# A mixture-of-experts block whose tokens are dispatched by lists: rows gathered by index, results added into an accumulator in DRAM

## The chip, the cores and the metric

The kernel runs on one core of a Trainium2 chip. The metric is the device time of one execution, in microseconds, as the median of several runs. The core has TensorE (PE), VectorE (DVE), ScalarE (ACT), GpSimd (POOL) and SyncE (SP), which run their own instruction streams and meet through semaphores. SP, ACT and POOL issue DMAs, which 16 DMA engines carry out.

## The reference, cut to what matters

```python
def grouped_moe(x, w_router, b_router, w_gate, w_up, w_down):
    bsz, s, d = x.shape
    xt = x.reshape(bsz * s, d)
    gates = shared_group_router(xt, w_router, b_router).astype(x.dtype)
    out = jnp.zeros_like(xt)
    for e in range(N_EXPERTS):
        h = jax.nn.silu(xt @ w_gate[e]) * (xt @ w_up[e])
        out = out + gates[:, e:e + 1] * (h @ w_down[e])
    return out.reshape(bsz, s, d)

def reference(...):
        ...
        x = layer_norm(DN_ALPHA * x + merged @ w_out[l], ln1_g[l], ln1_b[l])
        moe = grouped_moe(x, w_router, b_router, w_exp_gate[l], w_exp_up[l], w_exp_down[l])
        x = layer_norm(DN_ALPHA * x + moe, ln2_g[l], ln2_b[l])
```

There are 512 tokens of width 1024, 16 experts with a hidden width of 512, float32 throughout. The router picks two experts for each token, so a row of `gates` has two entries that aren't zero. DN_ALPHA is 2 to the power 1/4. Ahead of this stand an input projection, two token mixers (a short convolution and a linear recurrence) and an output projection; `x` after the first layer norm is `x1` below.

## The kernel before

Every float32 product is made of three matmuls: a weight is split into a high part (ScalarE copies it to float32r, `whi` or `ehi`) and a low part (VectorE subtracts, `wlo` or `elo`), the data likewise, and TensorE adds high by high, high by low and low by high. So each weight tile passes DMA, ScalarE, VectorE and TensorE in this order. Everything is written out by hand: each engine has its list, and the semaphores set what waits for what.

The kernel has four stages.

1. **Projections and mixers** (lines 533 to 625 on PE): 74 weight tiles stream through two buffers `wst`. Beside them, POOL zeroes two DRAM buffers `xs` and `ys` of 23 blocks of 128 rows (lines 459 to 467): first one block of `xs` after each finished weight tile, then the parts of `ys`, whose waits have long been met by then.
2. **Output projection, layer norm, router.** DVE works out for every token its two experts and gates, and `dest`, the row that it gets in block order (block b is expert b; a block is 128 rows; further blocks would hold what an expert has over 128). `warm` (line 648) is matmuls whose result is not used, put where TensorE would otherwise wait. The rows of block 0 are made on TensorE itself, by multiplying `x1` with columns of ones and zeros, `block0` (line 754). At the same time POOL scatters the rows of `x1` to `xs` at `dest` (line 471), eight DMAs of 512 KB each, waits for them and loads block 1 (line 488).
3. **Experts.** A turn of TensorE is `gate_up(b)`, `rows_t(b + 1)` (the transposes of the next block's rows, line 710), `down(b - 1)`, `hidden_t(b)`. The rows come through one buffer `xe`, and y leaves through one buffer `yb`. ACT's turn rounds the next expert's weights and copies y out of PSUM in two halves (`y_out`, line 1032, semaphore `y_evac`), each followed by a DMA to `ys`. SP loads six weight tiles of 1 MB for each expert (line 328), one buffer `est` for each of the six; a buffer is free when the low part is made. A block's first 80 rows (`HEAD`) are loaded and stored by two DMAs, the rest only where the expert has more than 80 tokens. POOL's queue in this stage is, for b from 3: `load_rows(b)`, which waits for the transposes of the block ahead (`xe_t`), then `store_rest(b - 3)`, which waits for `y_evac`.
4. **Combination and second layer norm.** After the last store, POOL gathers each token's two rows of `ys` (line 528), TensorE sums them with `x1` by diagonal matrices of the gates and of alpha (lines 791 and 796), DVE does the layer norm from PSUM (lines 1303 to 1332), and SP stores four tiles.

## Time and profile before

| | us |
|---|---|
| median of 3 runs | 893.28 |
| lowest, highest run | 891.27, 897.67 |
| span of the profiled execution | 895.1 |
| PE busy | 856.0 (96%) |
| DVE busy | 575.7 (64%) |
| ACT busy | 465.1 (52%) |
| POOL busy | 75.4 (8%) |
| share of PE in the chain of waits | 87% |
| share of DMA in the chain of waits | 5% |

The span runs from the first to the last instruction of the core in the one execution that was profiled. Nothing is shown for that execution but its span, so the span is held against the median. Busy time is time in which an engine executes; an engine with little of it can still hold up others by where a wait stands in its list. The kernel moved 195.87 MB by DMA.

### The profile page before, as it was taken

The numbers are of one execution on the slowest core, as the hardware profiler recorded it, in microseconds if no ns is written. First come the engines' busy times: TensorE is split into PE (matmuls) and PEld (weight loads), VectorE is DVE, ScalarE is ACT, GpSimd is POOL, SyncE is SP. The second block draws the span as 40 slices with busy tenths as digits, with TensorE's granted clock in tenths as the row PEclk, the third lists the DMA queues.
The fourth block names the chain that finished last, engine by engine and source line by source line (L and its number), as shares of the span: only waits on it lengthen the run. The fifth ranks groups of instructions, "written<-read, shape, count | busy, mean of one in ns | idle before, by whom it ended". The sixth has DMA issues, their size and how long they took to land.

```text
span 895.1 us, 12524 instructions
## 1 busy us (share of the span) xinstructions
PE 856.0 (96%) x4036; PEld 709.3 (79%) x4036; DVE 575.7 (64%) x626; ACT 465.1 (52%) x482; POOL 75.4 (8%) x137
## 2 busy tenths in 40 slices
PE   6999999979999999999999999899999999999993
PEld 5888788868888888888888988688888888888761
DVE  5778344334458874423544698478889889888727
ACT  3655543423566653422325541468787877778610
POOL 1100000500000000000000001401111110010040
PEclk8999999989999999999999998899999999999997
DMA  6565555972333335334229814699999999999753
GB/s 181 175 177 166 177 196 189 251 246 89 94 94 94 94 115 170 114 100 118 88 69 335 262 41 161 255 355 372 380 373 379 383 381 372 381 381 382 256 170 135
DMA packets 168097, 195.87 MB, mean 219 GB/s; under 512 B 7998, under 2 KB 106918, under 8 KB 168070
## 3 DMA queue, kind: packets, MB, share of 16 engines
q1 hardware_dynamic: 154374, 157.69, 52.6%
q0 software_dynamic: 10624, 32.57, 10.8%
q10 hardware_dynamic: 3072, 5.24, 1.6%
q8 instruction: 17, 0.28, 0.1%
q14 instruction: 10, 0.08, 0.0%
HBM read 164.94 MB, written 30.54 MB: 218 GB/s over the span
## 4 chain that ended last, share of the span: by engine, by line
PE 87%; DMA 5%; DVE 4%; ACT 1%; POOL 1%; issue 1%; ACTq 0%; SPq 0%; DVEq 0%; POOLq 0%
PE psA L553 7%; PE psA L554 7%; PE psA L555 7%; PE psA L722 6%; PE psA L724 6%; PE psA L723 6%; PE psB L553 6%; PE psB L555 6%; PE psB L554 6%; PE psB L743 3%; PE psB L745 3%; PE psB L744 3%; PE psB L648 2%; DMA wst<-in_w_in_dram 2%; PE psD L553 2%; PE psD L554 2%
## 5 line engine op out<-in xcount | busy, mean ns | idle before, releaser
L1282 DVE TENSOR_TENSOR elo<-est,ehi 128x2048 fp32r<-128x2048 f32 x94 | 211.6, 2288 | 37.1 <-ACT ehi L964 36.8
L964 ACT ACTIVATE ehi<-est 128x2048 fp32r<-128x2048 f32 x92 | 173.3, 1914 | 38.0 <-DMA est<-in_w_exp_down_dram 16.6
L1095 DVE TENSOR_TENSOR wlo<-wst,whi 128x1024 fp32r<-128x1024 f32 (+1 forms) x78 | 97.5, 1249 | 97.5 <-ACT whi L811 96.4
L811 ACT ACTIVATE whi<-wst 128x1024 fp32r<-128x1024 f32 (+1 forms) x78 | 83.9, 1077 | 93.8 <-PE psA L555 36.4
L722 PE MATMUL psA<-ehi,xe_hi 128*128 128x512 f32 x256 | 102.2, 399 | 1.5 <-DVE xe_lo L1479 1.5
L724 PE MATMUL psA<-ehi,xe_lo 128*128 128x512 f32 x256 | 100.6, 393 | 0.0
L723 PE MATMUL psA<-elo,xe_hi 128*128 128x512 f32 x256 | 100.4, 392 | 0.0
L553 PE MATMUL psB<-xT_hi,whi 128*128 128x512 f32 x208 | 80.9, 389 | 0.0
L554 PE MATMUL psB<-xT_lo,whi 128*128 128x512 f32 x208 | 80.9, 389 | 0.0
L555 PE MATMUL psB<-xT_hi,wlo 128*128 128x512 f32 x208 | 80.9, 389 | 0.0
L722 PEld LDWEIGHTS psA<-ehi,xe_hi 128*128 128x128 f32 x256 | 48.6, 190 | 12.0 <-DVE xe_lo L1479 2.2
L553 PE MATMUL psA<-xT_hi,whi 128*128 128x512 f32 x144 | 57.4, 398 | 0.0
L554 PE MATMUL psA<-xT_lo,whi 128*128 128x512 f32 x144 | 57.1, 397 | 0.0
L555 PE MATMUL psA<-xT_hi,wlo 128*128 128x512 f32 x144 | 57.0, 396 | 0.0
L724 PEld LDWEIGHTS psA<-ehi,xe_lo 128*128 128x128 f32 x256 | 48.5, 189 | 10.5
L723 PEld LDWEIGHTS psA<-elo,xe_hi 128*128 128x128 f32 x256 | 48.6, 190 | 9.8
L743 PE MATMUL psB<-ehi,hT_hi 128*128 128x512 f32 x128 | 52.0, 406 | 1.8 <-DVE hT_lo L1491 1.8
L745 PE MATMUL psB<-ehi,hT_lo 128*128 128x512 f32 x128 | 50.8, 397 | 0.0
L744 PE MATMUL psB<-elo,hT_hi 128*128 128x512 f32 x128 | 50.4, 393 | 0.0
L553 PEld LDWEIGHTS psB<-xT_hi,whi 128*128 128x128 f32 x208 | 39.0, 188 | 8.2
L554 PEld LDWEIGHTS psB<-xT_lo,whi 128*128 128x128 f32 x208 | 39.0, 188 | 8.2
L555 PEld LDWEIGHTS psB<-xT_hi,wlo 128*128 128x128 f32 x208 | 39.0, 188 | 8.0
(271 smaller groups left out, 1630.3 us busy)
## 6 DMA issues: line engine op xcount, KB each, us to landing
est<-in_w_exp_gate_dram SPq DMA_DIRECT2D x32, 1024.0 KB, 12.2
est<-in_w_exp_up_dram SPq DMA_DIRECT2D x32, 1024.0 KB, 10.6
est<-in_w_exp_down_dram SPq DMA_DIRECT2D x32, 1024.0 KB, 11.8
wst<-in_w_in_dram SPq DMA_DIRECT2D x60, 512.0 KB, 3.9
xs<-zero POOLq DMA_DIRECT2D x23, 512.0 KB, 2.9
wst<-in_w_out_dram SPq DMA_DIRECT2D x16, 512.0 KB, 5.2
wst<-in_w_branch_r_dram SPq DMA_DIRECT2D x8, 640.0 KB, 4.2
ys<-yb ACTq DMA_DIRECT2D x32, 160.0 KB, 5.1
```

Source lines behind the costliest of these rows:

```text
L553: pe.matmul(bank, s_hi[:, k, :], m_hi[:, k, :], start=(k == 0), stop=False)
L554: pe.matmul(bank, s_hi[:, k, :], m_lo[:, k, :], start=False, stop=False)
L555: mm = pe.matmul(bank, s_lo[:, k, :], m_hi[:, k, :], start=False, stop=(k == K - 1))
L722: pe.matmul(psA[s // 2], xe_hi[:, q, :], ehi[s][:, k, :], start=(q == 0), stop=False)
L723: pe.matmul(psA[s // 2], xe_hi[:, q, :], elo[s][:, k, :], start=False, stop=False)
L724: mm = pe.matmul(psA[s // 2], xe_lo[:, q, :], ehi[s][:, k, :], start=False, stop=(q == KD - 1))
L743: pe.matmul(psB[s], hT_hi[:, k, :], ehi[4 + s][:, k, :], start=(k == 0), stop=False)
L745: mm = pe.matmul(psB[s], hT_lo[:, k, :], ehi[4 + s][:, k, :], start=False, stop=(k == KF - 1))
L811: A(whi[p][:, 0:K, :], wst[p][:, 0:K, :], ACT.Copy).then_inc(w_hi, 1)
L964: A(ehi[s][:], est[s][:], ACT.Copy).then_inc(gu_hi if s < 4 else d_hi, 1)
L1095: V.tensor_tensor(wlo[p][:, 0:K, :], wst[p][:, 0:K, :], whi[p][:, 0:K, :], ALU.subtract).then_inc(w_lo, 1)
L1282: V.tensor_tensor(elo[s][:], est[s][:], ehi[s][:], ALU.subtract).then_inc(gu_lo if s < 4 else d_lo, 1)
```

## The change

The rows of `x1` are no longer copied into block order. SP stores `x1` once as it is, to `x1d`, and once more as the start of an accumulator `acc`. POOL scatters only pairs of 8 bytes, the token's number and its gate divided by alpha, to a table `tab`, and reads this back as `lists`, 128 rows by 23 blocks. Entries that no token has hold the number of a trash row beyond 511 and a gate of zero. The rows of a block are then gathered from `x1d` by the numbers in `lists`; numbers over 511 are skipped. ACT scales y by the gate as it copies it out of PSUM, and POOL adds all 128 rows of `yb` to the rows of `acc` with an indirect DMA whose operation is an addition. At the end `acc` is loaded as it is: it holds the residual and both experts' parts, all divided by alpha, which the epsilon of the second layer norm makes good. The zeroed buffers, the second gather and the sums on TensorE are gone.

The first two experts do not use the lists. DVE makes columns `chosen_by` for both, and TensorE multiplies them with the token numbers `tokid`, which gives `pick0`, the indices for the first two gathers. The core of the diff:

```diff
-    xs = nc.dram_tensor("xs", (BLOCKS * P, D), F32, kind="Internal").ap()
-    ys = nc.dram_tensor("ys", (BLOCKS * P, D), F32, kind="Internal").ap()
+    x1d = nc.dram_tensor("x1d", (S + P, D), F32, kind="Internal").ap()
+    acc = nc.dram_tensor("acc", (S + P, D), F32, kind="Internal").ap()
+    tab = nc.dram_tensor("tab", (BLOCKS * P, 2), I32, kind="Internal").ap()
...
-            for s in range(6):
+            for s in range(2):
+                load_expert(sp, 1, s)
+            for t in range(TT):
+                sp.wait_ge(x1_done, t + 1)
+                sp.dma_start(x1d[t * P:(t + 1) * P, :], x1[:, t, :]).then_inc(x1_stored, 16)
+            for s in range(2, 6):
                 if s == 5:
-                    sp.wait_ge(xe_landed, 32)
+                    sp.wait_ge(xe_landed, 16)
+                    for t in range(TT):
+                        sp.dma_start(acc[t * P:(t + 1) * P, :], x1[:, t, :]).then_inc(acc_seeded, 16)
...
+            sp.wait_ge(y_stored, (more + NE) * 16)
+            for t in range(TT):
+                sp.dma_start(xa[:, t, :], acc[t * P:(t + 1) * P, :]).then_inc(got[t], 16)
...
-            with pool.Fori(0, BLOCKS) as b:
-                pool.wait_ge(tile_done, b + 1)
-                pool.dma_start(xs[ds(b * P, P), :], zero[:]).then_inc(zero_done, 16)
-            with pool.Fori(0, NE) as b:
-                pool.wait_ge(tile_done, b + (BLOCKS + 1 - NE))
-                pool.dma_start(ys[ds(b * P + HEAD, P - HEAD), :], zero[HEAD:P, :]).then_inc(zero_done, 16)
-            with pool.Fori(NE, BLOCKS) as b:
-                pool.dma_start(ys[ds(b * P, P), :], zero[:]).then_inc(zero_done, 16)
...
+            for dram in (acc, x1d):
+                pool.dma_start(dram[S:S + P, :], zero[:]).then_inc(trash_zeroed, 16)
+            pool.dma_start(tab.rearrange("(b p) w -> p b w", p=P), vacant[:]).then_inc(tab_cleared, 16)
+            pool.wait_ge(tab_cleared, 16)
+            pool.wait_ge(trash_zeroed, 32)
+
+            def gather(idx, most=S - 1):
+                pool.indirect_dma_start(out=xe[:], out_offset=None, in_=x1d,
+                                        in_offset=bass.IndirectOffsetOnAxis(ap=idx, axis=0),
+                                        bounds_check=most, oob_is_err=False).then_inc(xe_landed, 16)
+
+            def scatter_add(idx, n_before):
+
+                pool.wait_ge(y_evac, n_before * 2 + 2)
+                if not (isinstance(n_before, int) and n_before == 0):
+                    pool.wait_ge(y_stored, n_before * 16)
+                pool.sem_inc(pool_step, 1)
+                pool.indirect_dma_start(out=acc, out_offset=bass.IndirectOffsetOnAxis(ap=idx, axis=0),
+                                        in_=yb[:], in_offset=None, compute_op=ALU.add).then_inc(y_stored, 16)
+
+            pool.wait_ge(x1_stored, 16 * TT)
+            pool.wait_ge(pick_done, 1)
+            gather(pick0[:, 0:1])
             pool.wait_ge(dest_done, 1)
-            for t in range(TT):
-                for n in range(2):
+            for n in range(2):
+                for t in range(TT):
                     pool.indirect_dma_start(
-                        out=xs, out_offset=bass.IndirectOffsetOnAxis(ap=dest[:, n, t:t + 1], axis=0),
-                        in_=x1[:, t, :], in_offset=None).then_inc(scat, 16)
-
+                        out=tab, out_offset=bass.IndirectOffsetOnAxis(ap=dest[:, n, t:t + 1], axis=0),
+                        in_=pick[:, n, t, :], in_offset=None).then_inc(scat, 16)
+                if n == 0:
+                    pool.wait_ge(xe_t, 1)
+                    pool.wait_ge(pick_done, 2)
+                    gather(pick0[:, 1:2])
             pool.wait_ge(scat, 16 * 2 * TT)
...
-            load_rows(1, first=True)
+            pool.dma_start(lists[:], tab.rearrange("(b p) w -> p b w", p=P)).then_inc(lists_landed, 16)
+            pool.wait_ge(lists_landed, 16)
+            pool.wait_ge(acc_seeded, 16 * TT)
+            for b in range(2, NE):
+                pool.wait_ge(xe_t, b)
+                gather(lists[:, b, 0:1].bitcast(U32))
+                scatter_add(lists[:, b - 2, 0:1].bitcast(U32), b - 2)
+            for b in range(NE - 2, NE):
+                scatter_add(lists[:, b, 0:1].bitcast(U32), b)
             pool.wait_ge(plan_done, 2)
-
-            load_rows(2)
-            with pool.Fori(3, NE) as b:
-                load_rows(b)
-                store_rest(b - 3)
-            for b in range(NE - 3, NE):
-                store_rest(b)
...
-            warm(8, psB[0])
-
-            pe.wait_ge(block0_done, 1)
-            for k in range(KD):
+            warm(4, psB[0])
+            for e in range(2):
+                pe.wait_ge(by_done, e + 1)
                 for t in range(TT):
-                    mm = pe.matmul(psC[0][:, k // 4, (k % 4) * P:(k % 4 + 1) * P],
-                                   x1[:, t, k * P:(k + 1) * P], block0[:, t, :],
+                    mm = pe.matmul(psA[e][:, 0:2], chosen_by[:, e, t, :], tokid[:, t, :],
                                    start=(t == 0), stop=(t == TT - 1))
-            mm.then_inc(xe_t, 1)
-            warm(11, psB[0])
+                mm.then_inc(pick_t, 1)
+            warm(24, psB[0])
+            rows_t(0)
+            warm(9, psB[0])
             gate_up(0, first=True)
             rows_t(1)
             hidden_t(0, first=True)
...
             def y_out(b, s, first=False):
                 act.wait_ge(d_used, b * 2 + (s + 1))
-                if not first:
-                    act.wait_ge(y_stored, b * 32)
-                    act.wait_ge(y_rest_stored, b * 32)
-                A(yb[:, s * DF:(s + 1) * DF], psB[s], ACT.Copy).then_inc(y_evac, 1)
-                dst = ys[b * P:(b + 1) * P, :] if isinstance(b, int) else ys[ds(act.snap(b * P), P), :]
-                act.wait_ge(y_evac, b * 2 + (s + 1))
-                act.dma_start(dst[0:HEAD, s * DF:(s + 1) * DF], yb[0:HEAD, s * DF:(s + 1) * DF]
-                              ).then_inc(y_stored, 16)
+                if first:
+                    act.wait_ge(lists_landed, 16)
+                else:
+                    act.wait_ge(y_stored, b * 16)
+                A(yb[:, s * DF:(s + 1) * DF], psB[s], ACT.Copy,
+                  scale=lists[:, b, 1:2].bitcast(F32)).then_inc(y_evac, 1)
 
...
+            for e in range(2):
+                ins = V.tensor_scalar(keys[:, e, :], sel[:, :, e], -1000.0, 1000.0, ALU.mult, ALU.add)
+            chain.link(ins)
 
             dve.wait_ge(pos_done, 1)
-            dve.wait_ge(sel_done, 1)
             cnt, ext, inc, bb = (r16[n][:, 0, :] for n in (9, 10, 11, 12))
             pos, row = r16[13], r16[14]
-            V.tensor_copy(pos[:], psB[1][:, 0:TT * NE].rearrange("p (t e) -> p t e", e=NE))
-            dve.wait_ge(picked0, 1)
-            V.tensor_scalar(key[:], k0[:], -1000.0, 1000.0, ALU.mult, ALU.add)
+            at_pos = psB[1][:, 0:TT * NE].rearrange("p (t e) -> p t e", e=NE)
+            for e in range(2):
+                V.tensor_tensor(keys[:, e, :], keys[:, e, :], at_pos[:, :, e], ALU.add).then_inc(key_done, 1)
+            for e in range(2):
+                dve.wait_ge(key_done, e + 1)
+                for t in range(TT):
+                    ins = V.tensor_scalar(chosen_by[:, e, t, :], slots[:], keys[:, e, t:t + 1], None, ALU.is_equal)
+                ins.then_inc(by_done, 1)
+            V.tensor_copy(pos[:], at_pos)
             chain.link(V.tensor_copy(cnt, psB[1][:, TT * NE:(TT + 1) * NE]))
-
-            tt(key[:], key[:], pos[:, :, 0], ALU.add)
-            for t in range(TT):
-                ins = V.tensor_scalar(block0[:, t, :], slots[:], key[:, t:t + 1], None, ALU.is_equal)
-            ins.then_inc(block0_done, 1)
...
             def summed(t):
-                dve.wait_ge(sum_done, t + 1)
-                moments([pairs[t][:, h, :] for h in range(2)], t % 2)
-                variance(t % 2, 1, 2 * TT + 2 * t + 2)
+                dve.wait_ge(got[t], 16)
+                moments(_halves(xa[:, t, :], S), t % 2)
+                variance(t % 2, 1, 2 * TT + 2 * t + 2, LN_EPS / ALPHA ** 2)
 
             summed(0)
             for t in range(TT):
                 if t + 1 < TT:
                     summed(t + 1)
                 rstd(t % 2, 1, 3 + t)
-                scale_rows(yg[:, 0, t, :], pairs[t][:].rearrange("p a s -> p (a s)"), t % 2, ln2_gb, out_ready)
+                scale_rows(xa[:, t, :], xa[:, t, :], t % 2, ln2_gb, out_ready)
```

On POOL, in the expert turns, before: the loop over b from 3. Ahead of these rows stands the load of the first 80 rows of a block with its wait for the transposes (L488). `full` is the flag for more than 80 rows.

```order
L492 ISA x2
L493 COMPARE_AND_BRANCH
L494 ISA
L494 DMA xe<-xs 48x1024
L493 UNCONDITIONAL_BRANCH
L495 COMPARE_AND_BRANCH
L496 ISA
L496 DMA xe<-xs 1x16x64
L495 UNCONDITIONAL_BRANCH
L500 ISA
L502 ISA [waits y_evac]
L502 DMA ys<-yb 16x1x64
```

The wait for y stands behind the load of rows and belongs to the block three before it.

On POOL, in the same place, now, with the end of the dispatch ahead of it; the gather is L493, the addition into `acc` L503.

```order
L493 DMA xe<-x1d,pick_106 128x1024 [waits pick_done,xe_t]
L512 DMA tab<-pick,dest 2944x2 x4
L520 DMA lists<-tab 128x23x2 [waits scat]
L493 DMA xe<-x1d,lists 128x1024 [waits xe_t,acc_seeded,lists_landed]
L503 DMA acc<-yb,lists 640x1024 [waits y_evac]
L493 DMA xe<-x1d,lists 128x1024 [waits xe_t]
L503 DMA acc<-yb,lists 640x1024 [waits y_evac,y_stored]
```

The loop is written out, and gather and addition alternate: gather of block 2, addition of block 0, gather of block 3, and so on. The wait for y belongs to the block two before.

On PE, at the dispatch, before: from the counts of the router to the first matmuls of expert 0.

```order
L700 MATMUL psB<-sel,ones_b 128x16 x4
L648 MATMUL psB<-ehi_163 128x512 x8
L754 MATMUL psC<-block_184,x_88 128x128 [waits block0_done]
L754 MATMUL psC<-block_184,x_88 128x128 x31
L648 MATMUL psB<-ehi_163 128x512 x11
L722 MATMUL psA<-ehi_163,xe_hi 128x512 [waits gu_lo,xe_l]
```

And now, in the same place:

```order
L704 MATMUL psB<-sel,ones_b 128x16 x3
L706 MATMUL psB<-sel,before_b 128x16
L708 MATMUL psB<-sel,ones_b 128x16 x4
L656 MATMUL psB<-ehi_167 128x512 x4
L762 MATMUL psA<-tokid,chosen_by 128x2 [waits by_done]
L762 MATMUL psA<-tokid,chosen_by 128x2 x3
L762 MATMUL psA<-tokid,chosen_by 128x2 [waits by_done]
L762 MATMUL psA<-tokid,chosen_by 128x2 x3
L656 MATMUL psB<-ehi_167 128x512 x24
L719 MATMUL psC<-ident,xe 128x128 [waits xe_landed]
L719 MATMUL psC<-ident,xe 128x128 x7
L656 MATMUL psB<-ehi_167 128x512 x9
```

Eight small matmuls take the place of 32, and block 0 now comes through a gather and the same transposes as the other blocks.

## Rows read from the trace of the kernel before

**Rows 1.** Chain of waits in order of time: start us, us, what.
```profile
592.96 0.87 PE psC L710 x8
...
823.49 0.87 PE psC L710 x8
```

**Rows 2.** Busy time in one stretch of the expert turns.
```profile
core 0: us, PE busy (x) PEld busy (x) DVE busy (x) ACT busy (x) POOL busy (x), PEclk, DMA share, GB/s
...
650.00:700.00 50.00, 50.00 (x241) 41.55 (x239) 45.57 (x26) 39.27 (x31) 4.98 (x10) 1.00 1.05 378
```

**Rows 3.** Tile est: landing of its loads, in 616 to 634, then 722 to 740.
```profile
DMA to landing us min/median/max: 7.8/9.3/10.6
...
DMA to landing us min/median/max: 11.9/12.9/13.9
```

**Rows 4.** Timeline, 179 to 202: start us, us, engine, what [idle before].
```profile
179.44 0.53 POOL L466 DMA_DIRECT2D ys<-zero  x1 [0.29 <-issue]
...
196.22 0.79 PE L553 MATMUL psC<-xT_hi,whi 128*128 128x512 f32 x1 [5.25 <-DVE wlo L1095]
...
201.83 0.40 PE L554 MATMUL psC<-xT_lo,whi 128*128 128x512 f32 x1
```

**Rows 5.** Chain of waits at the start of the kernel.
```profile
1.08 3.24 DMA x<-in_x_dram
```

**Rows 6.** Timeline at the dispatch.
```profile
551.83 0.87 DVE L1441 TENSOR_SCALAR block<-slots,r 128x128 f32<-128x128 f32 x4
...
552.96 7.30 PE L754 MATMUL psC<-block,x 128*128 128x128 f32 x64
```

**Rows 7.** Line 471, the scatters of x1: durations in ns, landing.
```profile
L471 POOL DMA_INDIRECT xs<-x,dest x8: 958/964/2337, 556.7 to 567.1; - x8
...
DMA to landing us min/median/max: 3.5/4.3/4.7
```

**Rows 8.** Timeline of PE between expert 0 and expert 1.
```profile
576.33 1.21 PE L710 MATMUL psC<-ident,xe 128*128 128x128 f32 x8 [2.47 <-DMA xe<-xs]
...
579.91 0.80 PE L722 MATMUL psA<-ehi,xe_hi 128*128 128x512 f32 x1 [1.52 <-DVE xe_lo L1479]
...
583.92 0.43 PE L722 MATMUL psA<-ehi,xe_hi 128*128 128x512 f32 x1
```

**Rows 9.** Timeline of POOL: the last scatter of x1, then a late turn.
```profile
567.06 0.96 POOL L471 DMA_INDIRECT xs<-x,dest  x1 [0.30 <-issue]
...
807.44 0.53 POOL L488 DMA_DIRECT2D xe<-xs  x1 [2.26 <-PE psC L710]
...
821.50 0.49 POOL L502 DMA_DIRECT2D ys<-yb  x1 [12.04 <-ACT yb L1032]
```

**Rows 10.** Timeline of PE and ACT in an early turn.
```profile
628.26 1.03 PE L710 MATMUL psC<-ident,xe 128*128 128x128 f32 x8
...
636.85 1.92 ACT L964 ACTIVATE ehi<-est 128x2048 fp32r<-128x2048 f32 x1 [0.59 <-ACT yb L1032]
638.67 0.58 ACT L1032 ACTIVATE yb<-psB 128x512 f32<-128x512 f32 x1
```

**Rows 11.** DMA issues: count, KB each, median us to landing.
```profile
xe<-xs POOLq DMA_DIRECT2D x15, 320.0 KB, 6.4
...
xe<-xs POOLq DMA_DIRECT2D x14, 4.0 KB, 5.3
```

**Rows 12.** Timeline of the tail.
```profile
856.44 0.60 ACT L1032 ACTIVATE yb<-psB 128x512 f32<-128x512 f32 x1 [2.29 <-PE psB L745]
...
857.32 0.48 POOL L502 DMA_DIRECT2D ys<-yb  x1 [5.22 <-ACT yb L1032]
...
870.99 1.29 DVE L1303 BATCH_NORM_STATS2 stat<-psC 128x6 f32<-128x512 f32 x2 [17.34 <-PE psC L796]
...
874.35 1.30 DVE L1303 BATCH_NORM_STATS2 stat<-psD 128x6 f32<-128x512 f32 x2 [1.64 <-PE psD L796]
```

More of the change, by code:

```diff
@@ L268, in trunk_moe @@
         plan_done = sem("plan_done")
-        zero_done = sem("zero_done")
+        trash_zeroed = sem("trash_zeroed")
+        tab_cleared = sem("tab_cleared")
+        x1_stored = sem("x1_stored")
+        acc_seeded = sem("acc_seeded")
+        key_done = sem("key_done")
+        by_done = sem("by_done")
+        pick_t = sem("pick_t")
+        pick_done = sem("pick_done")
         scat = sem("scat")
+        lists_landed = sem("lists_landed")
+        cur_landed = sem("cur_landed")
         dve_step = sem("dve_step")
@@ L521, in _ @@
                 with pool.Fori(0, more) as i:
-                    load_rows(i + NE)
-                    store_rest(i + NE)
-            pool.wait_ge(all_stored, 1)
-            for t in range(TT):
-                for n in range(2):
-                    pool.indirect_dma_start(
-                        out=yg[:, n, t, :], out_offset=None, in_=ys,
-                        in_offset=bass.IndirectOffsetOnAxis(ap=dest[:, n, t:t + 1], axis=0)
-                    ).then_inc(got[t], 16)
+                    pool.wait_ge(y_stored, (i + NE) * 16)
+                    pool.wait_ge(xe_t, i + NE)
+                    pool.dma_start(cur[:], tab[ds(i * P + NE * P, P), :]).then_inc(cur_landed, 16)
+                    pool.wait_ge(cur_landed, i * 16 + 16)
+                    pool.sem_inc(pool_step, 1)
+                    gather(cur[:, 0:1].bitcast(U32), None)
+                    scatter_add(cur[:, 0:1].bitcast(U32), i + NE)
         @block.tensor
@@ L705, in rows_t @@
             def rows_t(b):
-                pe.wait_ge(xe_landed, b * 32)
-                pe.wait_ge(xe_l, b)
+                pe.wait_ge(xe_landed, b * 16 + 16)
+                if not (isinstance(b, int) and b == 0):
+                    pe.wait_ge(xe_l, b)
                 for k in range(KD):
@@ L782, in _ @@
                     down(i + NE)
-            pe.wait_ge(diag_done, 1)
-            for t in range(TT):
-                if t == TT - 1:
-                    pe.wait_ge(y_evac, (more + NE) * 2)
-                    warm(18, psB[0])
-                for h in range(2):
-                    pe.matmul(pairs[t][:, h, :], alpha_i[:], x1[:, t, h * S:(h + 1) * S], start=True, stop=False)
-            for t in range(TT):
-                pe.wait_ge(got[t], 32)
-                for n in range(2):
-                    for h in range(2):
-                        mm = pe.matmul(pairs[t][:, h, :], diag[:, n, t, :], yg[:, n, t, h * S:(h + 1) * S],
-                                       start=False, stop=(n == 1))
-                mm.then_inc(sum_done, 1)
         @block.scalar
@@ L1054, in _ @@
             turn(1, first_prev=True)
-            with act.Fori(2, NE - 1) as b:
+            for b in range(2, NE - 1):
                 turn(b)
@@ L1077, in _ @@
                     hidden_round(b)
-                    for s in range(2):
-                        y_out(b, s)
-            act.wait_ge(y_stored, (more + NE) * 32)
-            act.wait_ge(y_rest_stored, (more + NE) * 32)
-            A(stat[:, 40:41], stat[:, 30:31], ACT.Copy).then_inc(all_stored, 1)
+                    act.wait_ge(d_used, b * 2 + 2)
+                    act.wait_ge(y_stored, b * 16)
+                    A(yb[:], pairs[3][:].rearrange("p a s -> p (a s)"), ACT.Copy,
+                      scale=lists[:, ds(b, 1), 1].bitcast(F32)).then_inc(y_evac, 2)
             for t in range(TT):
@@ L1377, in red @@
                 chain.link(V.tensor_reduce(o, a, AX, op))
-            k0, key = r1[3], r1[4]
             ex, iota3 = r16[1], iota_e[:].unsqueeze(1).to_broadcast([P, TT, NE])
```

96 lines of the change are left out of this document (37 added, 59 removed).

## The prediction

> **What bounds the kernel now.** I read the chain of waits first: from the transposes of the gathered rows (line 710) of block 2 to those of block 15 it lies on TensorE alone, 592.96 to 823.49 us, 13 turns of one expert each, so 17.73 us a turn [rows 1]. The DMA engines are the second limit and close: in that stretch their share is 1.05 at 378 GB/s [rows 2], and a weight load takes a median of 9.3 us to land at 616 to 634 us but 12.9 at 722 to 740 [rows 3]. That is six turns, so the queue falls behind by 0.6 us a turn: a turn's transfers need 18.3 us against TensorE's 17.7. A turn moves six weight loads of 1.049 MB, 0.33 MB of rows in and 0.33 MB of y out, 6.95 MB; over 18.3 us that is 379 GB/s, the rate just read. ScalarE and GpSimd have room, but GpSimd's queue has an order that matters below. The time is judged against the span of the profiled execution, 895.1 us; the median of the runs is 893.3, so I take 1.8 off at the end.
>
> **Zeroing goes.** The last zero writes of xs and ys are issued in one burst up to 179.44 us, and a weight load behind them makes TensorE idle for 5.25 us before 196.22; it comes back at half clock, so that 13 matmuls up to 201.83 take 5.61 us instead of 13 x 0.23 = 2.99 [rows 4]. Worth 5.25 + 2.62 = 7.9 us, all on the chain, since the tiles that follow only queue behind. The two zero writes and the table clear that replace it come at the start, beside the load of x; they could hold that up by some tenths of a us, at most by its own 3.24 [rows 5], and I take 0.
>
> **Dispatch of experts 0 and 1.** The 32 small matmuls that selected rows for block 0 ran 7.30 us from 552.96, behind key columns finished at 551.83 + 0.87 [rows 6]. Now VectorE makes eight such columns instead of four (to about 553.5), four tiny matmuls and one add give the indices (553.8), and GpSimd gathers: nearest row the scatters of x1, landing in 3.5 to 4.7 us [rows 7], so at 557.5 to 558.5. The 24 warm matmuls cover that (553.5 + 24 x 0.23 = 559.0), then transposes 1.0, copy 1.0 and subtract 1.2 as before: expert 0 starts within 0.5 us of where it did. I take 0. The extra gate and key operations on VectorE lie in the time in which 30 warm matmuls run, and cost nothing. For expert 1 the eight 512 KB scatters of x1 no longer stand ahead of the row load: the index gather is issued around 562 and has 11 us. TensorE's wait of 2.47 us before 576.33 goes, and with it the half clock after it, in which nine matmuls from 579.91 to 583.92 took 4.01 us instead of 2.07 [rows 8]: 2.5 + 1.9 = 4.4 us. The 1.52 us wait for the low part stays. Bounds: block 2's gather waits for eight table scatters and for the lists, 128 x 23 entries of 8 bytes, an access of a kind that no row shows. By my count the gather goes out at about 580 and is needed at 588; if the lists take 5 us more, nothing of the gain is left, if 8 more it is a loss of 3. The four stores of x1 run while the queue is empty, and the four seeds of the accumulator take 2.1 MB / 379 GB/s = 5.5 us at 558 to 564, while the buffers of expert 2 aren't free yet.
>
> **The expert turns, the term that decides.** GpSimd's queue now reads gather(b), scatter_add(b-2), gather(b+1). scatter_add(b-2) waits for ScalarE's second copy of y (`y_evac`), and everything behind it on GpSimd waits too: the next gather, and through it TensorE's next transposes. Before, the row load went out right after the transposes (GpSimd at 807.44) and the wait for y came behind it (12.04 us, until 821.50), so a whole turn hid the load [rows 9]. Now there is a ring around each turn:
> - transposes start to second y copy end: 628.26 to 638.67 + 0.58 = 10.99 us, less the 0.59 that ScalarE waits around its own DMA issue, which goes: 10.4 [rows 10]. Late in the phase it is longer, as ScalarE waits for weights there; if turns get longer it waits less, so 10.4.
> - copy end to GpSimd's start: 856.44 + 0.60 to 857.32, 0.3 [rows 12].
> - GpSimd's issue of the scatter-add and the gap: 0.96 + 0.30 = 1.26 [rows 9].
> - the gather's landing under the load of weights: direct row loads take 5.3 us for 4 KB and 6.4 for 320 KB [rows 11], 3.5 ns per KB; 64 rows (1024 chosen rows over 16 experts) are 256 KB, 6.2 us. It stands behind the scatter-add of 128 rows, 512 KB, in the same queue: 1.8 us if each byte passes once, 3.6 if the old value is fetched as well, less the 1.26 of head start: 6.7 or 8.5 us.
> Sum 18.7 or 20.5 us, against TensorE's 17.73. No row shows a transfer that adds. One that costs nothing extra and one that costs twice are the nearest bounds; I take twice, since old and new value must both be read. The DMA side says the same: 6.29 + 0.26 + 0.52 = 7.08 MB is 18.7 us a turn, with the second read 7.60 MB and 20.1 us. So a turn of **20.5 us**, with TensorE idle some 2.8 us before each row of transposes. Thirteen rings lie between block 2 and block 15: 13 x 2.77 = +36.0 us. If the idle time also brings the half clock, as 2.47 us did [rows 8], the first down matmuls end later and a turn can reach 22.7.
>
> **The tail.** Before: y copied at 857.04, small y stores, then eight gathers, sums on TensorE, and VectorE's first statistics at 870.99, its second at 874.35 after waiting for TensorE [rows 12]. Now the last scatter-add starts at 857.3 and lands after about 4.4 (the scatters' median 4.3 [rows 7]), SP loads four 512 KB tiles, the first in about 3.2 (x at the start, 3.24 [rows 5]), so statistics start at 865.0. VectorE's own work is 895.1 - 874.35 = 20.75 plus 1.7 for the first pair: end at 887.5, **7.6 us** earlier. Between 4 (a slow add) and 9.
>
> **A rule against my count.** The row loads above took 5.3 us even for 4 KB while the weights streamed. The Trainium skill, DMA: Bandwidth & Descriptors, section Anatomy of one DMA — SWDGE (gpsimd) path, gives a GpSimd-issued transfer about 2.0 us fixed plus its bytes at 436 GB/s. An estimate by it is 2.6 us for the gather and a ring below TensorE's turn, so no stall at all. The 5.3 us row disagrees with it under load, and the 3.5 us row comes near it when the queue is quiet.
>
> **Sum.** 895.1 - 7.9 - 4.4 - 7.6 = 875.2 without the ring; + 36.0 = 911.2; less 1.8 gives **909 us**, +1.8%.
>
> **The rivals.**
> 1. *No stall.* The gather lands as fast as in a quiet queue, 3.5 us: the ring is 10.4 + 0.3 + 1.3 + 3.5 = 15.5, TensorE stays the bound, and the DMA's lag of 1 us a turn is taken up by the margin that lets 9.4 us landings grow to 13 without a stall. 875.2 - 1.8 = **873 us**, faster. For it: DMA would have idle time if turns grow. Against it: share 1.05 in every stretch. Chance 0.2.
> 2. *The add costs no second pass.* Ring 18.7 us, +12.6: **886 us**, just short of 1% faster. Chance 0.22.
> 3. *Twice the bytes*, the forecast, 900 to 920: chance 0.4.
> 4. *The add is slower still, or the half clock follows each stall*: 22.7 us a turn, +64.6: **938 us**. Chance 0.18.
> The scatter-add doesn't decide while the ring stays under 17.73 us; with 12.0 us spent up to the gather's issue that leaves 5.7 us for its landing. At 19.2 us a turn the gains elsewhere are used up and the kernel is slower than before.
>
> **How the numbers follow.** The forecast is case 3's. Some 1% is what a measurement of this kernel can tell from no change (the runs lie within 0.7%). Faster by over 1% (below 884.4) is case 1 and a few of case 2: 0.23. Within 1% (to 902.2) is most of case 2 and the lower edge of case 3: 0.24. Slower: 0.53. The range goes from 875, which takes in most of case 1, to 940; case 3 alone is 900 to 920.
>
> **What the profile after would show.** TensorE idle before each of the transposes of block 3 to 15, released by the DMA of the gathered rows; GpSimd idle before the scatter-adds, released by the y copy, with the gather right behind; turns of about 20.5 us; the DMA share of the expert phase below 1.0 if the ring binds, still above it if the doubled bytes do. No gap at 190 us. Statistics starting some 8 us after the last y copy. I am wrong if the gather lands within 5.7 us of its issue, if an added row costs far more than a second read, or if the lists arrive late and hold block 2.

## The result, and the profile after

The changed kernel takes a median of 989.81 us (987.04 to 994.62), the kernel before beside it 893.29: ratio 1.109, 95% interval [1.106, 1.112]. I had forecast 909, with a range of 875 to 940. The profiled execution has a span of 986.4 us, 91.3 more than before.

The windows of the trace after: the gap at 190 us is closed, and in the expert turns TensorE is busy 196 of 250 us, at a mean clock of 0.87 of the upper level and with DMA engines that are no longer full, where [rows 2] had 50.00 of 50 and a share of 1.05.

```profile
core 0: us, PE busy (x) PEld busy (x) DVE busy (x) ACT busy (x) POOL busy (x), PEclk, DMA share, GB/s
180.00:200.00 20.00, 20.00 (x90) 16.56 (x89) 7.06 (x8) 6.10 (x8) 0.00 (x0) 1.00 0.36 105
600.00:850.00 250.00, 195.66 (x821) 160.38 (x820) 155.16 (x89) 138.26 (x107) 46.50 (x20) 0.87 0.82 278
```

What TensorE waited for (us in total, times, longest us): the gather of rows once in each turn, and an early wait that was 3.5 us before.

```profile
PE psC L719 <- DMA xe<-x1d,lists: 69.5, 14, 6.7
PE psB L553 <- DVE xT_lo L1090: 12.1, 1, 12.1
```

The timeline of PE, at the places that cut the kernel in four: the selection matmuls, the transposes of block 2 and of block 15.

```profile
546.76 0.18 PE L706 MATMUL psB<-sel,before_b 128*128 128x16 bf16 x1 [1.72 <-DVE sel L1412]
586.51 1.09 PE L719 MATMUL psC<-ident,xe 128*128 128x128 f32 x8 [0.83 <-DMA xe<-x1d,lists]
914.26 1.57 PE L719 MATMUL psC<-ident,xe 128*128 128x128 f32 x8 [4.60 <-DMA xe<-x1d,lists]
```

The first of these before, in the same view:

```profile
550.67 0.18 PE L698 MATMUL psB<-sel,before_b 128*128 128x16 bf16 x1
```

The transposes of [rows 1] stand in this view at 592.80 and 823.33, 0.16 us ahead of the pieces of the chain. With them and the spans, the 91.3 us split without a remainder: up to the selection matmuls 550.67 - 546.76 = 3.9 us gained; from there to block 2, 42.1 before and 39.8 now, 2.4 gained; block 2 to block 15, 230.5 before and 327.75 now, **97.2 lost**, a turn of 25.2 us instead of 17.73; from block 15 to the end 71.8 and 72.1, 0.4 lost. My terms for these were -7.9, -4.4, +36.0 and -7.6.

One ring, from the chain of waits (start us, us, what): transposes at half clock (granted 0.50 in 737.7 to 739.6), ScalarE's rounding of weight tiles and the second y copy, the scatter-add's issue, the gather's landing, the next transposes. It is the ring of the prediction, with all its parts.

```profile
737.69 1.98 PE psC L719 x8
...
740.62 2.37 ACT ehi L957 x2
...
746.71 1.80 ACT ehi L957
748.51 0.58 ACT yb L1026
...
749.90 3.01 POOL acc L503
752.91 0.31 issue
753.22 9.37 DMA xe<-x1d,lists
762.59 0.04 issue
762.63 1.97 PE psC L719 x8
```

The start, on ACT: the first weight tile of the projections arrives at 19.82 us. The DMA issues of the page show what stood in front of it.

```profile
19.82 1.06 ACT L804 ACTIVATE whi<-wst 128x1024 fp32r<-128x1024 f32 x1 [8.37 <-DMA wst<-in_w_in_dram]
```
```profile
acc<-zero POOLq DMA_DIRECT2D x1, 512.0 KB, 7.7
x1d<-zero POOLq DMA_DIRECT2D x1, 512.0 KB, 11.2
...
tab<-vacant POOLq DMA_DIRECT2D x1, 23.0 KB, 17.4
```

The tail, timeline of all engines:

```profile
943.53 2.36 POOL L503 DMA_INDIRECT acc<-yb,lists  x1 [14.45 <-ACT yb L1026]
...
952.35 1.27 ACT L1026 ACTIVATE yb<-psB,lists 128x512 f32<-128x512 f32 x2 [9.64 <-DMA acc<-yb,lists]
...
954.42 1.55 POOL L503 DMA_INDIRECT acc<-yb,lists  x1 [8.53 <-ACT yb L1026]
...
964.11 1.29 DVE L1293 BATCH_NORM_STATS2 stat<-xa 128x6 f32<-128x512 f32 x2 [19.65 <-DMA xa<-acc]
```

### The profile page after: what moved, and what is told of

Same layout as the page of the kernel before. It is cut to its first block, busy times and chain, and to the rows that moved or that the text cites. A ratio compares the mean times of both kernels' runs of the same rounds, so it can differ in the third digit from the quotient of the medians.

```text
span 986.4 us, 11507 instructions
## 1 busy us (share of the span) xinstructions
PE 850.9 (86%) x3940; PEld 708.6 (72%) x3940; DVE 575.3 (58%) x622; ACT 465.9 (47%) x481; POOL 92.5 (9%) x62
## 4 chain that ended last, share of the span: by engine, by line
PE 56%; DMA 19%; ACT 7%; issue 6%; POOL 5%; DVE 5%; SPq 0%; ACTq 0%; POOLq 0%; DVEq 0%
DMA xe<-x1d,lists 14%; PE psA L561 7%; PE psA L562 7%; PE psA L563 7%; PE psB L561 6%; PE psB L562 6%; PE psB L563 6%; ACT ehi L957 5%; POOL acc L503 4%; PE psC L719 3%; DMA wst<-in_w_in_dram 2%; PE psB L752 2%; PE psB L753 2%; PE psB L754 2%; DMA acc<-yb,lists 2%
## 5 line engine op out<-in xcount | busy, mean ns | idle before, releaser
L1006 ACT ACTIVATE xe_hi<-psC 128x1024 fp32r<-128x1024 f32 x16 | 16.4, 1025 | 156.9 <-PE psC L719 156.9
L719 PE MATMUL psC<-ident,xe 128*128 128x128 f32 x128 | 28.4, 395 | 69.5 <-DMA xe<-x1d,lists 69.5
L1475 DVE TENSOR_TENSOR xe_lo<-psC,xe_hi 128x1024 fp32r<-128x1024 f32 x16 | 19.6, 1225 | 104.3 <-ACT xe_hi L1006 104.3
L719 PEld LDWEIGHTS psC<-ident,xe 128*128 128x128 f32 x128 | 22.7, 205 | 75.6 <-DMA xe<-x1d,lists 75.4
L503 POOL DMA_INDIRECT acc<-yb,lists x16 | 43.9, 2744 | 301.3 <-ACT yb L1026 301.3
L752 PE MATMUL psB<-ehi,hT_hi 128*128 128x512 f32 x128 | 60.2, 471 | 1.8 <-DVE hT_lo L1487 1.8
L753 PE MATMUL psB<-elo,hT_hi 128*128 128x512 f32 x128 | 57.3, 447 | 0.0
L754 PE MATMUL psB<-ehi,hT_lo 128*128 128x512 f32 x128 | 56.7, 443 | 0.0
```

What stands on the lines that cost most here:

```text
L503: pool.indirect_dma_start(out=acc, out_offset=bass.IndirectOffsetOnAxis(ap=idx, axis=0), in_=yb[:], in_offset=None, compute_op=ALU.add).th ...
L719: mm = pe.transpose(psC[0][:, k // 4, (k % 4) * P:(k % 4 + 1) * P], xe[:, k * P:(k + 1) * P], ident[:])
```

## The experiments

Ratios are to the kernel before on the same chip. Where a kernel ran once only (e2, e3, e5, e6, e7), its span is held against 986.4; four executions of the changed kernel had spans of 985.3 to 993.0, so a difference of a few us says little by itself. The table at the end of this section splits the spans by stage.

**e1_ahead** takes the ring away by the order alone.

```diff
                 gather(lists[:, b, 0:1].bitcast(U32))
-                scatter_add(lists[:, b - 2, 0:1].bitcast(U32), b - 2)
-            for b in range(NE - 2, NE):
+                if b > 2:
+                    scatter_add(lists[:, b - 3, 0:1].bitcast(U32), b - 3)
+            for b in range(NE - 3, NE):
```

> Only the order on GpSimd changes: gather(b) now stands ahead of the scatter-add of block b-3, so no gather waits for y any more. The ring theory says that TensorE stops waiting for rows before each block's transposes, and the turn falls from 25.1 us to whatever comes next. Next is either TensorE (17.73 us, if the DMA engines have time left: total about 890 us) or the DMA engines. Their busy share in the changed kernel is 0.83 of a 25.1 us turn, against a share of 1.05 when they are full, so a turn's transfers need 0.85 x 25.1 / 1.05 = 20.3 us: total 905 to 925 us. I take the second. The rival, that the transfers that add are slow in themselves and the order does little, gives over 960 us.

911.65 us, 1.020 [1.015, 1.025], in the expected range. The 14 waits for the gather became one of 6.8 us. The order is worth 1.1088 - 1.0197 = 8.9% of 893 us, 79.6 us. What then bounds the turns is the DMA queue: TensorE waits behind weights (`hT_lo` follows a rounded weight tile in VectorE's list, and ScalarE waits for the weights themselves), and the share is back over 1.

```profile
600.00:840.00 240.00, 228.72 (x1071) 187.65 (x1070) 197.92 (x113) 176.80 (x138) 51.37 (x25) 1.00 1.04 361
```
```profile
PE psB L753 <- DVE hT_lo L1488: 15.4, 10, 4.9
...
PE psC L720 <- DMA xe<-x1d,lists: 6.8, 1, 6.8
...
ACT ehi L958 <- DMA est<-in_w_exp_up_dram: 31.3, 10, 3.6
```

**e2_plain** drops `compute_op=ALU.add`: y overwrites rows of `acc`, the addition of the experts is left out.

> The indirect scatter of y overwrites rows instead of adding to them (the addition is left out, so the output is that of the last writer); order and bytes written stay. If the addition costs a second read of each byte, the gather behind it lands 2 to 3 us earlier and a turn falls from 25.1 to about 22 us: about 950 us. If the addition is nearly all of the cost, the gather lands in 6.5 us instead of 9.4 to 10 and GpSimd issues it in 1 us instead of 3: about 925 us. The rival, that only place in the queue and waiting for VectorE count, leaves 980 to 990 us.

Span 964.2, 22 us shorter, between the first range and the rival; the scatter's issue has a median of 2363 ns instead of 2996. A turn takes 23.9 us instead of 25.2, so leaving the addition out returns 17 of the 97 us. The gather behind it lands only 0.5 us earlier (9.3 us after its start instead of 9.7, means of 13 turns). Another 9.0 us went behind block 15. In the chains of waits the adding transfers of blocks 14 and 15, then the plain ones of e2:

```profile
943.53 8.74 DMA acc<-yb,lists
...
954.42 6.13 DMA acc<-yb,lists
```
```profile
928.76 4.38 DMA acc<-yb,lists
...
935.31 3.31 DMA acc<-yb,lists
```

The packets and bytes of the software queue are the same, its time is not: 6.1% of 986.4 us against 3.9% of 964.2, 60.2 and 37.6 us of all 16 engines. That is 22.6 us for 16 additions of 512 KB, 1.4 us each, and 512 KB at the 379 GB/s of the prediction are 1.4 us: the addition takes the engines' time of one more pass.

```profile
q0 software_dynamic: 5280, 14.33, 6.1%
```
```profile
q0 software_dynamic: 5280, 14.33, 3.9%
```

**e3_skip** adds `bounds_check=S - 1, oob_is_err=False` to the scatter-add, so that empty entries are skipped (1024 rows of 4 KB in all).

> The scatter-add skips the entries without a token (bounds 511), so it moves 64 rows on average instead of 128; the ring stays. If the size of the add sets the gather's landing, the turn falls by half of what the add costs in the ring, 2 to 3 us of 25.1: 950 to 965 us. If a fixed price or the issue on GpSimd sets it, it stays at 980 to 990 us.

Span 980.9, 5.5 us shorter, as the second range had it: the turn is 25.0 us instead of 25.2, and the gather lands after 9.5 us instead of 9.7. With a ring, bytes matter little.

**e4_ahead_skip** has e1's and e3's edits.

> Both: gather ahead of the scatter-add, and only rows with tokens are added. A turn's transfers are then 6.29 MB of weights, 0.26 MB of rows and 0.26 MB of added rows, each of these perhaps for two. If adding costs twice its bytes or less, that is 7.1 MB and 18.5 to 18.7 us a turn, near TensorE's 17.73, and the queue's margin hides most of it: 875 to 890 us, faster than the kernel before. If added rows cost several times their bytes, the DMA engines stay the bound: 895 to 910 us.

906.79 us, 1.016 [1.011, 1.022], in the range of the second case. Without the ring the kernel is still slower than before; TensorE's ten waits for `hT_lo` stay (14.9 us).

**e5_short_lo** asks why the scatter-add's issue takes 3 us.

```diff
-                V.tensor_tensor(elo[s][:], est[s][:], ehi[s][:], ALU.subtract).then_inc(gu_lo if s < 4 else d_lo, 1)
+                n = 4 if s < 4 or isinstance(b, int) and b == 0 else 1
+                V.tensor_tensor(elo[s][:, 0:n, :], est[s][:, 0:n, :], ehi[s][:, 0:n, :],
+                                ALU.subtract).then_inc(gu_lo if s < 4 else d_lo, 1)
```

> The kernel after with VectorE's low parts of the down weights cut to a quarter from block 1 on (three quarters of those 30 subtractions are left out, and so is their share of the result); all transfers and all matmuls are the same. Theory: GpSimd's issue of the scatter-add (2996 ns median, 1552 where VectorE is idle) and of the gather (1.95 us, 1.07 quiet) is held up while VectorE runs its 2.3 us subtractions, so with three quarters of two of them gone in each turn the scatter-add's issue falls towards 1.6 to 2.3 us, and the turn of 25.2 us gets 1 to 2 us shorter: span 960 to 975. Rival: the issue is long for another reason (the accumulation, the load on the DMA engines): 2996 stays within 100 ns and the span within 984 to 988.

Span 974.9, at the theory's upper edge. The lists came late in this execution (TensorE waited 7.9 us for block 2 instead of 0.83), which hides part of the gain: a turn takes 23.96 us instead of 25.21, 16.3 us over thirteen. The lines of the scatter-add in the kernel after and in e5 (ns min/median/max): with no subtraction beside it, all sixteen take what the last one took before.

```profile
L503 POOL DMA_INDIRECT acc<-yb,lists x16: 1552/2996/3074, 597.8 to 954.4; - x16
```
```profile
L503 POOL DMA_INDIRECT acc<-yb,lists x16: 1552/1580/1643, 608.0 to 942.7; - x16
```

The gather's issue moved the other way, from a median of 1.95 us to 3.14, since VectorE's next two subtractions now lie beside it; it still lands 9.7 us after its start, so this cost the ring nothing. The timeline of e5: beside the scatter-add VectorE has only the rest of a small `hT_lo`, beside the gather's 3.14 us the 2.29 us of a subtraction.

```profile
751.41 0.69 DVE L1489 TENSOR_TENSOR hT_lo<-psD,hT_hi 128x512 fp32r<-128x512 f32 x1 [0.37 <-ACT hT_hi L1018]
...
751.71 1.58 POOL L503 DMA_INDIRECT acc<-yb,lists  x1 [19.02 <-ACT yb L1026]
...
753.53 2.29 DVE L1273 TENSOR_TENSOR elo<-est,ehi 128x2048 fp32r<-128x2048 f32 x1 [1.43 <-ACT ehi L957]
...
753.59 3.14 POOL L493 DMA_INDIRECT xe<-x1d,lists  x1 [0.31 <-issue]
```

The `hT_lo` has one of its two inputs in PSUM; it overlaps the scatter-add by 0.39 us and lengthens it by nothing.

**e6_warm** puts 48 small matmuls with an unused result in front of the transposes of blocks 3 to 15.

> The kernel after with 48 matmuls of 128 columns added in front of the row transposes of each block from 3 on, in a bank that nobody reads, in the time in which TensorE waits for the gather. Theory: in the turns the granted clock is 0.87, since TensorE waits 5 us in each; kept busy it stays at 1.00, the 10.4 us from the transposes to the y copy that I took from the turns before the change come true instead of 11.4, and the turn falls from 25.2 to 24.2 us, the span to 971 to 976. Rival: the added matmuls are in the way of the landed rows, or the clock is not what lengthens that part: 984 to 995.

Span 983.9, 2.5 us shorter and at the rival's edge, though the clock in 600 to 850 us rose from 0.87 to 0.95. But the span doesn't decide this: the added matmuls kept the clock up in some turns only, and block 2's rows came later than in the kernel after (a wait of 3.9 us instead of 0.83). Two turns of e6, from the chain of waits, transposes to second y copy:

```profile
715.32 1.11 PE psC L722 x8
...
725.16 0.69 ACT yb L1029
...
739.71 1.97 PE psC L722 x8
...
750.75 0.68 ACT yb L1029
```

In five of the thirteen turns the transposes took 1.09 us, as at full clock; there that part of the ring is 10.5 to 10.8 us. In four they took 1.92 or 1.97, and it is 11.4 to 11.7; in the kernel after twelve of thirteen are of this kind. So where full clock was kept, the predicted 10.4 came nearly true, and the average turn fell by 0.45 us, to 24.76. The rest of that part, 9.4 us at either clock, lies on ScalarE, whose list has three rounded tiles ahead of the first copy and a fourth ahead of the second.

**e7_late_clear** has one added line, `pool.wait_ge(tile_done, 8)`, ahead of the three clearing DMAs.

> The kernel after, with one thing moved: GpSimd starts the clearing of the list table (2944 entries of 8 bytes), and of the 128 spare rows of both buffers, after the eighth weight tile instead of in the first 6 us. Theory: in the changed kernel the table's clear (17.4 us to its landing) lies in front of the first weights, which land at 19.82 us where they landed at 11.08 before, and the channel constants come 8.7 us later; with the clear moved both come back, and the span falls from 986.4 to 976 to 979. Rival: the start is bound by the loads of x itself and the delay has another source: the span stays within 984 to 988, and the first weights still land near 20 us.

Span 978.6, 7.8 us shorter; the transposes of the constants' rows, which waited 12.1 us, start at 14.56 instead of 23.41. The theory holds. Whether it is the table's 2944 pieces or the 1 MB of zeroes was not separated.

**e8_ahead_skip_late** has all three edits.

> The kernel after with three edits: each gather is queued ahead of the scatter-add of three blocks earlier (not two), empty entries are skipped in the scatter-add by a bound, and the clearing is started after the eighth tile. The first two alone gave 906.8. Theory: the start's 8 to 9 us add to that: 897 to 900, so still 0.4 to 1% behind the kernel before, since the turns are bound by the DMA engines, whose traffic the addition has raised. Rival: the later start of all that follows was hidden by something in the middle: 904 to 908.

901.84 us, 1.010 [1.008, 1.012]; two us above the theory's range and two below the rival's, still behind the kernel before.

**e12_ahead_copy** is e8 without the addition (left out, as in e2).

> The version with the gather queued ahead, empty entries skipped and the late clearing (901.8 us), with the scattered rows written over acc instead of added (the addition of the experts is left out). Theory: its turns are bound by the DMA engines (share 0.98 at 339 GB/s where the kernel before moves 367), and the addition, which reads what it adds to, is what they lack: TensorE's 13.3 us of waits for hT_lo go, 888 to 893. Rival: the indirect writing of 4 KB rows through the one software queue costs this in any form: 898 to 902.

885.74 us, 0.990 [0.986, 0.994]: below the range. The queue section and the weight loads of e8, then of e12, have the same packets and bytes; the software queue's time goes from 4.5% of 906.0 to 3.3% of 883.8, so 40.8 to 29.2 us of all 16 engines, and each weight load lands earlier.

```profile
q0 software_dynamic: 5280, 10.14, 4.5%
...
est<-in_w_exp_gate_dram SPq DMA_DIRECT2D x32, 1024.0 KB, 14.4
est<-in_w_exp_up_dram SPq DMA_DIRECT2D x32, 1024.0 KB, 13.6
```
```profile
q0 software_dynamic: 5280, 10.14, 3.3%
...
est<-in_w_exp_gate_dram SPq DMA_DIRECT2D x32, 1024.0 KB, 12.8
est<-in_w_exp_up_dram SPq DMA_DIRECT2D x32, 1024.0 KB, 10.0
```

TensorE's 13.3 us of waits for `hT_lo` fall to 3.0. Beside the other three edits the addition costs 1.0098 - 0.9901 = 2.0%, 17.6 us, and without it nothing of the loss is left. Not all of that is the full queue: of the 22.2 us between the two profiled spans, 11.1 lie in the turns (18.76 us each, then 17.91) and 9.8 behind block 15, where the last additions are waited for one after the other.

**e9_rows_back** is half of the change: dispatch by lists, but y stored to `ys` and combined as before; late clearing, and the zeroes of `ys` at one transfer a weight tile.

> Half of the change: the dispatch by lists of token numbers, with rows gathered from x1d, as in the kernel after; y is stored into the zeroed row buffer ys and summed at the end by diagonal matrices, as in the kernel before; the clearing is started after the eighth tile, and the zeroes of ys go out one transfer per weight tile, with none in a burst. Theory: the accumulator and the order it forces cost all of the loss; the dispatch by lists alone is a gain: 893.3 less 3.9 us at the selection matmuls, less the 8.7 us of the start, less 4.4 at the dispatch gives 876, range 873 to 880. Rival: the gathers of whole rows in 4 KB pieces cost more in the turns, which the DMA engines bound, than the plain loads of 80 rows they replace: 885 to 895.

882.77 us, 0.991 [0.988, 0.993]: between the theory's range and the rival's. TensorE waits 5.9 us for the gather of block 2, since the lists' read takes 7.3 us here (4.7 in the kernel after).

**e10_paced_zeroing** is the kernel before with its 46 zero writes spread over the first 29 tiles.

```diff
-                pool.wait_ge(tile_done, b + 1)
-                pool.dma_start(xs[ds(b * P, P), :], zero[:]).then_inc(zero_done, 16)
...
+            for b in range(BLOCKS):
+                pool.wait_ge(tile_done, b + 1 + max(0, b - NE))
+                pool.dma_start(xs[b * P:b * P + P, :], zero[:]).then_inc(zero_done, 16)
+                r0 = HEAD if b < NE else 0
+                pool.dma_start(ys[b * P + r0:b * P + P, :], zero[r0:P, :]).then_inc(zero_done, 16)
```

> The kernel before with one thing changed: the same zeroes are written, two transfers per weight tile at most, from the first tile on, so that no burst of them stands in front of the branch products. Theory: of the change's gain by having no zeroed buffers, 5.3 us was the idle time of TensorE behind that burst and some 2 the clock after it; pacing alone brings that back: 885 to 888. Rival: the traffic is moved into tiles whose weights then come late, or the clock at the start costs it back: 891 to 895.

885.14 us, 0.992 [0.990, 0.994], in the expected range. The gap at 190 us is gone here too, and the selection matmuls start at 539.36 instead of 550.67: the same zeroes, in another order, give most of what the change took from leaving them out.

**e11_first_lists** is e9 with the lists of blocks 2 and 3 read first.

```diff
-            pool.dma_start(lists[:], tab.rearrange("(b p) w -> p b w", p=P)).then_inc(lists_landed, 16)
+            entries = tab.rearrange("(b p) w -> p b w", p=P)
+            pool.dma_start(lists[:, 2:4, :], entries[:, 2:4, :]).then_inc(lists_landed, 16)
```

> The version with the new dispatch and the rows stored back (882.8 us) with its read of the lists split: first the entries of blocks 2 and 3 (256 pieces of 8 bytes), and those of the other blocks behind the first gather. Theory: TensorE's 5.9 us wait for the gather of block 2 is the table's way round (eight scatters of 8 bytes a row, 2944 pieces read back in 7.3 us beside expert weights); 256 pieces are back in 3 to 5 us, so 2 to 4 us of the wait go: 879 to 881. Rival: the landing is set by the load on the queues and not by the number of pieces, or the time is taken back by the DMA-bound turns behind it: 882 to 884.

883.89 us, 0.988 [0.985, 0.992]. That median lies in the rival's range; but the medians of different chips can't be held against each other, and the intervals of e9 and e11 overlap, so whether the wait's end shows in the time stays open. The POOL timeline of e11 shows the piece itself: the gather goes out 3.14 us after the start of the lists' read, and TensorE's wait is gone.

```profile
571.93 0.80 POOL L539 DMA_DIRECT2D lists<-tab  x1 [5.40 <-DMA tab<-pick,dest]
575.07 1.05 POOL L503 DMA_INDIRECT xe<-x1d,lists  x1 [2.34 <-DMA lists<-tab]
```

**e13_add_first_lists** is e8 with the lists of blocks 0 to 3 read first; **e14_rows_back_again** is e11 and **e15_paced_again** is e10, all three on one chip.

> The version with the accumulator that lost least (gather ahead, empty entries skipped, late clearing; ratio 1.0098), with its read of the lists split, blocks 0 to 3 first. Theory: the 7.1 us wait for the gather of block 2 goes as it went with the rows stored back, but the turns behind it are bound by the DMA engines with the addition in them, so that only a part shows: 895 to 900, still not ahead of the kernel before. Rival: all 7 us show, 892 to 895.

> The dispatch by lists with the rows stored back, paced zeroes and the split read of the lists, again, beside the kernel before with paced zeroes. Theory: the dispatch by lists gains the 4.4 us that I gave it, of which 2 to 4 show: it is 0.2 to 0.5% ahead of the paced one. Rival: it gains nothing of its own, and both are equal within 0.15%.

> The kernel before with its zeroes paced, again, beside the dispatch by lists with rows stored back. Theory: 885 to 887, 0.2 to 0.5% behind that one. Rival: equal within 0.15%.

e13: 897.41 us, 1.007 [1.005, 1.009]. e14: 881.30, 0.989 [0.987, 0.991]. e15: 884.40, 0.993 [0.991, 0.996]. So the accumulator's best form stays behind the kernel before; the dispatch by lists alone is 3.1 us ahead of the paced kernel before, with intervals that just touch; e11's kernel, run again as e14, is the fastest that keeps the whole computation.

The profiled executions by stage, in us, from the PE timelines:

| run | selection to block 2 | a turn, blocks 2 to 15 | block 15 to the end |
|---|---|---|---|
| before | 42.1 | 17.73 | 71.8 |
| after | 39.8 | 25.21 | 72.1 |
| e1, order | 43.8 | 18.89 | 75.5 |
| e2, no addition | 41.8 | 23.90 | 63.1 |
| e3, empty entries skipped | 39.5 | 24.99 | 69.3 |
| e5, short subtractions | 45.4 | 23.96 | 68.1 |
| e6, added matmuls | 42.7 | 24.76 | 71.2 |
| e8, order, skip, late clear | 44.6 | 18.76 | 75.1 |
| e12, e8 without addition | 44.6 | 17.91 | 65.2 |

## Why the prediction was wrong

**The direction and the mechanism were right, the sizes were not.** The step that failed is the turn of 20.5 us, 13 x 2.77 = +36.0. It measured 25.2, 13 x 7.48 = +97.2. Each part of the ring was priced too low. The ring of 24.94 us at 737.69 against the prediction's parts:

| part | predicted | measured |
|---|---|---|
| transposes to the end of the second y copy | 10.4 | 11.4 |
| copy end to GpSimd's start | 0.3 | 0.8 |
| scatter-add's issue and the gap | 1.26 | 3.32 |
| gather, issue to landing | 8.5 | 9.37 |

Over the thirteen turns the means are 11.5, 0.8, 3.2 and 9.7. The largest error is the issue, 2.1 us. I took 0.96 from a scatter of x1 in [rows 9] and passed over the maximum of 2337 ns in [rows 7]; that scatter started at 558.08, inside a subtraction of VectorE that ran for 2.28 us from 557.27. Of the 2.1, the addition gives about 0.6 (1545 ns against 976, the shortest in e8 and in e12) and VectorE's subtractions the rest, which e5 shows.

The 1.0 us in the first row is nearly all the clock. I took transposes at full clock from [rows 10]; behind a wait of some 5 us they run at half clock, 1.97 us instead of 1.09 (e6). My fourth rival named this, but priced it with the scatter-add at 22.7 us a turn, where the clock is worth about 1 us and the turn was 25.2.

The landing came near its 8.5 partly by luck. I built it from 6.7 and 1.8 for the second pass; without the addition it is 9.3 (e2), with half the rows 9.5 (e3). The base was too low by 2.6 us, and what the second pass adds too high by 1.3.

The price of the order was right in kind: it costs 79.6 us (e1). Once the ring is gone, the queue that fills up and the additions at the end keep every version that adds into the accumulator at 1.007 or more.

**Twice the bytes.** As the engines' time this was right: 1.4 us for 512 KB (after against e2), as the prediction's DMA side had it (18.7 and 20.1 us a turn), and 11.6 us for 16 times 256 KB (e8 against e12), 0.7 each. Both come from shares with one decimal, so they are good to about 1 us in total. What was wrong is where it hurts: little in the gather's landing, more on a full queue and in the tail.

**The zeroes.** The gap's 7.9 us went, and up to the selection 4.7 more: behind the earlier stream the wait before 493 us is 1.3 instead of 2.8, and the clock in 540 to 550 us 0.97 instead of 0.68. But the start, which I gave "at most its own 3.24", took 8.7 (the transposes of the constants' rows at 23.41 instead of 14.68). e7 returned 7.8 of it. And e10 shows that most of this gain needed no change of the data's way.

**The dispatch.** -4.4 predicted, -2.4 measured. The wait of 2.47 went, but expert 0 began 13.3 us behind the selection matmuls instead of 12.0, for which I had taken 0, and TensorE idled 0.83 for block 2. The lists came just in time only with the read at 4.7 us, in a stretch with a DMA share of 0.50. In e1, e8 and e9, where it fell beside weight loads (0.84 in e1), it took 7.3 to 8.6, and TensorE waited 5.9 to 7.1; in e2, e5 and e12 it was 7.0 to 8.5 and 3.2 to 7.9. These are the late lists that the prediction named as a risk.

**The tail.** -7.6 predicted, +0.4 measured. This term failed too. From the last scatter-add's start to the end it is 32.0 us against 37.8 from the last store's issue [rows 12], 5.8 gained. Ahead of it I had missed a wait: ScalarE can't write `yb` for block 15 before the scatter-add of block 14 has landed, 9.64 us. Transposes of block 15 to the last scatter's start are 40.2 us against 34.0. Behind both stands the addition: I had priced its landing at the 4.4 us of a plain scatter, and it took 8.7 and 6.1. Without it (e2) the stretch is 63.1 us, 8.7 less than before, near what I had forecast.

**The price of a quiet queue.** An estimate by the Trainium skill, DMA: Bandwidth & Descriptors, section Anatomy of one DMA — SWDGE (gpsimd) path, had the gather land in some 2.6 us; beside the stream of weights it took 9.4. The trace speaks against using that figure there.

## What to carry to other kernels

Before a wait is moved ahead of a load in one queue, write the ring it closes, and price each part at the slow end of its rows: in a ring every part counts. A maximum far above the median, like the 2337 ns of [rows 7], asks what ran beside that one instruction. Read the turns from the trace as well as the span: in e5 and e6 a late block 2 hid part of what the edit did. Undo the order first when such a change fails; here one line of order was worth 80 us and the new operation 18 to 22. And where a gain comes from work that disappears, try the same work in another place: pacing the zeroes gave 0.7% by itself.

## What the hardware showed that I had not expected

- VectorE holds up GpSimd's issue of DMAs: the indirect scatter-add takes 1.58 us without a subtraction beside it and 3.0 beside fp32 subtractions with both inputs in SBUF (e5). The Trainium skill, SBUF — State Buffer, section Who interferes with whom, says that a `tensor_copy` stalled such DMAs and a `tensor_tensor` did not, and calls its reason inferred; this case disagrees. The rule beside it in that section, that a VectorE instruction with two SBUF inputs contends with a GpSimd instruction that reads SBUF and one with at most one does not, fits both kinds of rows in e5.
- A clear of 23 KB in pieces of 8 bytes took 17.4 us to land, and with two 512 KB writes beside it delayed the first weights by 8.7 us. 23 KB read back in such pieces took 4.7 us at a DMA share of 0.50, 7.3 to 8.6 beside weights; 256 pieces landed in 2.4 (e11).
- An indirect DMA with an addition takes 1.55 us to issue at best, where the same without it takes 0.98. Its 16 engines are busy as for one more pass, 1.4 us for 512 KB. At the end of the kernel it landed in 8.7 and 6.1 us, without the addition in 4.4 and 3.3 (e2).
- Half the rows in front of a gather hardly change when it lands (9.7 and 9.5 us, e3). With no scatter of y in front it took 7.0 (e9).
